# Mixer projections of two layers as three reduced-precision products each, their weights split in place, with the time step apart and some loads and softmax steps reordered

## The reference

```python
for l in range(DEPTH):                       # DEPTH = 2
    x = x + 0.5 * swiglu_ffn(rms_norm(x, ffn1_norm[l]), ffn1_w_in[l], ffn1_w_out[l])
    h = rms_norm(x, mix_norm[l])             # [256, 1024]
    uv, c_q, c_kv, k_rope, z, xbc, dt_raw, gates = jnp.split(h @ w_in[l], IN_OFFSETS, axis=-1)
    y_a = gmlp_mixer(uv, ...)                # u, v: 512 columns each
    y_b = mla_mixer(c_q, c_kv, k_rope, ...)  # 384, 256, 32 columns; 8 heads, causal softmax
    y_c = ssd_mixer(z, xbc, dt_raw, ...)     # 512, 1024, 8 columns
    g = jax.nn.sigmoid(gates).reshape(bsz, s, 3, 1024)
    merged = g[:, :, 0] * (y_a @ w_branch[l, 0]) + g[:, :, 1] * (y_b @ w_branch[l, 1]) + g[:, :, 2] * (y_c @ w_branch[l, 2])
    x = x + merged @ w_out[l]
    x = x + 0.5 * swiglu_ffn(rms_norm(x, ffn2_norm[l]), ffn2_w_in[l], ffn2_w_out[l])
```

## Time and profile before

| | us |
|---|---|
| median of 3 runs (1914.6 to 1919.06) | 1916.91 |
| the profiled execution | 1915.92 |
| its span | 1914.2 |
| mixers of layer 0, u done to the last plain gate (224 to 404) | 180 |
| the same in layer 1 (893 to 1074) | 181 |

### The profile page before, as it was taken

The page is one execution under the profiler, slowest core; times in us unless marked ns, Lnnn a source line. Parts: engine busy times, 40 slices in busy tenths (PEclk is TensorE's granted clock), DMA queues, the critical chain, the costliest instruction groups (busy, mean ns, idle before and its releaser), DMA issues.

```text
span 1914.2 us, 25859 instructions
## 1 busy us (share of the span) xinstructions
PE 1863.4 (97%) x10920; PEld 1537.3 (80%) x10920; DVE 932.7 (49%) x1168; ACT 708.7 (37%) x815; POOL 78.0 (4%) x145
## 2 busy tenths in 40 slices
PE   8999999998999999999999988999999999999998
PEld 8998585567999899985855677998887975759996
DVE  4545124468555445451344683546677531235553
ACT  5544113153554345441131533555123121215542
POOL 0000000000000000000000002000371100000000
PEclk9999999999999999999999999999998999999999
DMA  7547244333655645562444338646344223326471
GB/s 242 176 170 245 64 144 157 129 126 119 220 176 186 222 142 176 184 232 64 142 156 132 127 116 155 234 144 246 109 141 93 66 69 130 133 88 220 131 260 59
DMA packets 192248, 293.07 MB, mean 153 GB/s; under 512 B 7219, under 2 KB 126805, under 8 KB 192165
## 3 DMA queue, kind: packets, MB, share of 16 engines
q1 hardware_dynamic: 189908, 287.72, 44.5%
q0 software_dynamic: 1936, 4.14, 2.1%
q10 hardware_dynamic: 320, 0.01, 0.0%
HBM read 289.49 MB, written 2.36 MB: 152 GB/s over the span
## 4 chain that ended last, share of the span: by engine, by line
PE 91%; DVE 4%; ACT 2%; issue 2%; DMA 1%; SPq 0%; ACTq 0%; DVEq 0%
PE acc L224 17%; PE acc L225 17%; PE acc L226 17%; PE acc L193 15%; PE acc L270 7%; PE acc L205 3%; PE acc L2460 1%; PE acc L2768 1%; PE acc L456 1%; PE acc L252 1%; PE acc L1206 1%; ACT big L1323 1%; DMA ring<-in_ffn_w_out 1%; PE acc L2163 1%; ACT part_hi L215 1%
## 5 line engine op out<-in xcount | busy, mean ns | idle before, releaser
L224 PE MATMUL acc<-xT_hi,w_hi 128*128 128x256 f32 x1680 | 476.8, 284 | 8.9 <-issue 8.5
L225 PE MATMUL acc<-xT_lo,w_hi 128*128 128x256 f32 x1680 | 476.0, 283 | 0.0
L226 PE MATMUL acc<-xT_hi,w_lo 128*128 128x256 f32 x1680 | 476.0, 283 | 0.0
L424 DVE TENSOR_TENSOR w_lo<-ring,w_hi 128x2048 fp32r<-128x2048 f32 x160 | 361.8, 2290 | 222.7 <-ACT w_hi L420 222.7
L420 ACT ACTIVATE w_hi<-ring 128x2048 fp32r<-128x2048 f32 x160 | 301.2, 1912 | 160.6 <-PE acc L226 98.1
L224 PEld LDWEIGHTS acc<-xT_hi,w_hi 128*128 128x128 f32 x1680 | 323.2, 192 | 9.7 <-issue 8.7
L225 PEld LDWEIGHTS acc<-xT_lo,w_hi 128*128 128x128 f32 x1680 | 323.2, 192 | 0.0
L226 PEld LDWEIGHTS acc<-xT_hi,w_lo 128*128 128x128 f32 x1680 | 323.1, 192 | 0.0
L193 PE MATMUL acc<-ring,xT 128*128 128x512 f32 (+2 forms) x672 | 274.6, 567 | 0.8 <-DVE xT L2748 0.8
L193 PEld LDWEIGHTS acc<-ring,xT 128*128 128x128 f32 x672 | 127.3, 191 | 138.0 <-issue 125.5
L224 PE MATMUL acc<-w_hi,hT_hi 128*128 128x512 f32 x440 | 172.4, 392 | 0.1
(11 more groups left out here) (507 smaller groups left out, 2121.6 us busy)
## 6 DMA issues: line engine op xcount, KB each, us to landing
ring<-in_ffn_w_in SPq DMA_DIRECT2D x88, 1024.0 KB, 5.7
ring<-in_w_in SPq DMA_DIRECT2D x48, 1024.0 KB, 5.1
ring<-in_ffn_w_out SPq DMA_DIRECT2D x44, 1024.0 KB, 6.4
ring<-in_w_branch SPq DMA_DIRECT2D x12, 1024.0 KB, 4.9
ring<-in_w_out SPq DMA_DIRECT2D x12, 1024.0 KB, 5.0
ring<-in_w_gate SPq DMA_DIRECT2D x11, 1024.0 KB, 5.3
ring<-in_w_up SPq DMA_DIRECT2D x11, 1024.0 KB, 6.5
ring<-in_w_down SPq DMA_DIRECT2D x11, 1024.0 KB, 6.1
```

Source lines behind the costliest of these rows:

```text
L224: pe.matmul(o, a_hi, wh, start=start, stop=False)
L225: pe.matmul(o, a_hi, wl, start=False, stop=False)
L226: return pe.matmul(o, a_lo, wh, start=False, stop=stop)
L424: vec.tensor_tensor(w_part(w_lo, r), raw_part(c0, r), w_part(w_hi, r).bitcast(F32), ALU.subtract).then_inc(f.lo, 1)
```

## The change

In both layers v, c_q, c_kv, xbc, z and gates 0 to 4 are no longer plain products but `three`. For this

- ACT copies the high part of each of 20 chunks (`early_act`) into one of four slots of `early_hi`, from gate 0 on into one of three of `gate_hi`; DVE writes the rest over the raw weights (`early_vec`). Gate 4 goes the way that gate 5 went (`gate_pe`, `part_hi`), so that two more chunks do.
- The high part of the input (`normed_hi`) is made at the start of the mixers instead of before the last gate, in the memory of `xn`; its rest is written over `xT` after u and the time step are done, so both of these stay plain. For v the products with the high part of the input stand ahead of those with its rest (`early_first_pe`).
- The 8 columns of the time step come by a load of their own (`dt_in`, a sixteenth in `params_sync`), and `dt_pe` stands right behind u.
- ACT and DVE steps are cut up and put in another order round the splits; the squares of the attention's norm go from DVE to ACT (`qs_squares_act`); `qs_vec5(1)` stands right behind `qs_vec5(0)`, ahead of two splits and a gate product.
- POOL's loads wait for the 8th high part of FFN2, and the four large ones for the 11th, 14th, 17th and 20th.

The diff, cut:

```diff
-        part_hi = over_big("part_hi", 21056, RING, 4, 512)
-        normed_hi = over_big("normed_hi", 19008, KD, TOK)
+        part_hi = over_big("part_hi", 21504, RING, 4, 512)
+        normed_hi = nc.alloc_sbuf_tensor_at("normed_hi", [P, KD, TOK], F32R, offset=xn_at)
+        early_hi = over_big("early_hi", 14912, RING, 2048)
+        gate_hi = [over_big(f"gate_hi{i}", off, 2048) for i, off in enumerate((14912, 16960, 6144))]
+        dt_in = sb("dt_in", [P, KD, 8])
...
-            C_SPLIT = C_GATE + 10
+            C_SPLIT = C_GATE + 8
...
+                sync.dma_start(dt_in[:, :, :], lay("w_in", l)[:, :, COLS["dt"]:COLS["dt"] + 8]
+                               .rearrange("o (k p) n -> p (o k) n", p=P)).then_inc(par_in, 16)
...
+            early = Counters(hi=sem(f"early_hi_ready{l}"), lo=sem(f"early_lo_ready{l}"))
+            EARLY = [(c + i, n) for c, n in ((C_V, 512), (C_CQ, QR), (C_KV, KVR + ROPE), (C_XBC0, 512), (C_XBC1, 512), (C_Z, 512),
+                                             *((C_GATE + 2 * g, 512) for g in range(4))) for i in range(2)]
+            N_PROJ = 12
...
+            def early_part(e):
+                hi = early_hi[:, e % RING] if e < N_PROJ else gate_hi[(e - N_PROJ) % 3]
+                n = EARLY[e][1]
+                return hi[:, 0:4 * n].rearrange("p (k n) -> p k n", k=4)
+            def early_act(act, *es):
+                for e in es:
+                    c, n = EARLY[e]
+                    wait_chunk(act, c)
+                    if e == 1:
+                        wait_products(act, C_MIX - 1)
+                    if e == N_PROJ + 2:
+                        act.wait_ge(gm.pe, 4)
+                    if e >= N_PROJ:
+                        wait_products(act, c - 3 if e >= N_PROJ + 3 else C_XBC1 + 1)
+                    act.activation(early_part(e), slot(c, 4, n), ACT.Copy).then_inc(early.hi, 1)
+            def early_vec(vec, *es):
+                for e in es:
+                    c, n = EARLY[e]
+                    vec.wait_ge(early.hi, e + 1)
+                    vec.tensor_tensor(slot_lo(c, 4, n), slot(c, 4, n), early_part(e).bitcast(F32), ALU.subtract).then_inc(early.lo, 1)
+            def early_chunk_pe(pe, G, m, e, i, products=None):
+                c, n = EARLY[e]
+                pe.wait_ge(early.lo, e + 1)
+                if i == 0 and products != 1:
+                    wait_acc_free(pe, G, m)
+                o, ms = acc[bank(G, m)][:, 0:n], slice(m * P, (m + 1) * P)
+                for k in range(4):
+                    xh, xl = normed_hi[:, 4 * i + k, ms], xT_rest[:, 4 * i + k, ms]
+                    wh, wl = early_part(e)[:, k, :], slot_lo(c, 4, n)[:, k, :]
+                    if products == 0:
+                        pe.matmul(o, xh, wh, start=(i == 0 and k == 0), stop=False)
+                        pe.matmul(o, xh, wl, start=False, stop=False)
+                    elif products == 1:
+                        ins = pe.matmul(o, xl, wh, start=False, stop=(i == 1 and k == 3))
+                    else:
+                        ins = three(pe, o, xh, xl, wh, wl, i == 0 and k == 0, i == 1 and k == 3)
+                if m == MT - 1 and products != 0:
+                    ins.then_inc(products_done, 1)
+            def early_group_pe(pe, G, e):
+                for i in range(2):
+                    for m in range(MT):
+                        early_chunk_pe(pe, G, m, e + i, i)
+            def early_first_pe(pe, G, e):
+                pe.wait_ge(tail.act, 1)
+                for i in range(2):
+                    for m in range(MT):
+                        early_chunk_pe(pe, G, m, e + i, i, 0)
+                pe.wait_ge(tail.vec, 1)
+                for i in range(2):
+                    for m in range(MT):
+                        early_chunk_pe(pe, G, m, e + i, i, 1)
+            def early_turned_pe(pe, G, e):
+                for i in range(2):
+                    c, n = EARLY[e + i]
+                    pe.wait_ge(early.lo, e + i + 1)
+                    for f in range(4):
+                        fs, o = slice(f * P, (f + 1) * P), acc[bank(G, f // 2)][:, (f % 2) * TOK:(f % 2 + 1) * TOK]
+                        if i == 0 and f % 2 == 0:
+                            wait_acc_free(pe, G, f // 2)
+                        for k in range(4):
+                            ins = three(pe, o, early_part(e + i)[:, k, fs], slot_lo(c, 4, n)[:, k, fs], normed_hi[:, 4 * i + k, :],
+                                        xT_rest[:, 4 * i + k, :], i == 0 and f % 2 == 0 and k == 0, i == 1 and f % 2 == 1 and k == 3)
+                    ins.then_inc(products_done, 1)
...
-                w_in(C_XBC1, "xbc1", 520)
+                w_in(C_XBC1, "xbc1", 512)
...
+                pe.wait_ge(dts.vec, 2)
...
-            def dt_pe(pe, m):
-
-                pe.wait_ge(cq.vec, 6)
-                for k in range(KD):
-                    ins = pe.matmul(turn[m][:, 0:8], xT[:, k, m * P:(m + 1) * P],
-                                    slot(C_XBC1 + k // 4, 4, 520)[:, k % 4, 512:520], start=(k == 0), stop=(k == KD - 1))
-                ins.then_inc(dts.pe, 1)
-
-            def dt_vec(vec):
+            def dt_pe(pe):
+
+                for m in range(MT):
+                    for k in range(KD):
+                        ins = pe.matmul(turn[2 + m][:, 0:8], xT[:, k, m * P:(m + 1) * P], dt_in[:, k, :], start=(k == 0), stop=(k == KD - 1))
+                    ins.then_inc(dts.pe, 1)
...
             def normed_act(act):
-                act.wait_ge(sd.pe, 11)
+                act.wait_ge(mix_norm.vec, mix_norm.turned(3))
                 act.activation(normed_hi[:, :, :], xT[:, :, :], ACT.Copy).then_inc(tail.act, 1)
-                act.wait_ge(qs.vec, 23)
-                act.wait_ge(sd.vec, 24)
-                act.wait_ge(sd.pe, 13)
             def normed_vec(vec):
                 vec.wait_ge(tail.act, 1)
-                wait_products(vec, C_SPLIT - 1)
+                wait_products(vec, C_U + 1)
+                vec.wait_ge(dts.pe, 2)
                 vec.tensor_tensor(xT_rest[:, :, :], xT[:, :, :], normed_hi[:, :, :].bitcast(F32), ALU.subtract).then_inc(tail.vec, 1)
+            def tail_slots_act(act, n):
+                if n == 0:
+                    act.wait_ge(qs.vec, 23)
+                    act.wait_ge(sd.vec, 20)
+                    act.wait_ge(sd.pe, 13)
+                else:
+                    act.wait_ge(sd.vec, 26)
...
-                group_pe(pe, G_V, C_V, xT, (4, 4), 512)
-                group_pe(pe, G_CQ, C_CQ, xT, (4, 4), QR)
+                dt_pe(pe)
+                early_first_pe(pe, G_V, 0)
+                early_group_pe(pe, G_CQ, 2)
                 gm_mix_pe(pe)
-                group_pe(pe, G_KV, C_KV, xT, (4, 4), KVR + ROPE)
-                turned_group_pe(pe, G_XBC0, C_XBC0, xT, 4, 512)
+                early_group_pe(pe, G_KV, 4)
+                early_turned_pe(pe, G_XBC0, 6)
                 cq_pe(pe)
-                turned_group_pe(pe, G_XBC1, C_XBC1, xT, 4, 520, between=dt_pe)
+                early_turned_pe(pe, G_XBC1, 8)
                 gm_turn_pe(pe)
-                group_pe(pe, G_Z, C_Z, xT, (4, 4), 512)
+                early_group_pe(pe, G_Z, 10)
                 sd_cs_pe(pe)
                 qs_groups_pe(pe)
                 sd_rows_pe(pe)
-                gate_pe(pe, 0)
+                early_group_pe(pe, G_GATE, 12)
                 sd_turn_pe(pe)
-                gate_pe(pe, 1)
+                early_group_pe(pe, G_GATE + 1, 14)
                 sd_y_pe(pe)
-                gate_pe(pe, 2)
+                early_group_pe(pe, G_GATE + 2, 16)
                 sd_off_pe(pe)
-                gate_pe(pe, 3)
+                early_group_pe(pe, G_GATE + 3, 18)
                 sd_out_pe(pe)
                 qs_turn_pe(pe)
                 gate_pe(pe, 4)
                 qs_scores_pe(pe)
-                pe.wait_ge(tail.vec, 1)
-                for i in range(2):
-                    for m in range(MT):
-                        ins = split_chunk_pe(pe, tail, G_GATE + 5, m, C_SPLIT + i, i, normed_hi[:, 4 * i:4 * i + 4],
-                                             xT_rest[:, 4 * i:4 * i + 4], part_hi, i == 0, i == 1)
-                    ins.then_inc(products_done, 1)
+                gate_pe(pe, 5)
...
-                gm_act(act)
-                cq_act(act)
+                early_act(act, 0)
+                normed_act(act)
+                early_act(act, 1)
+                gm_act(act, G_U, C_U, u_s)
+                early_act(act, 2, 3)
+                gm_act(act, G_V, C_V, v_s)
+                gm_norm_act(act)
+                early_act(act, 4, 5)
+                cq_act(act, 0)
+                early_act(act, 6, 7)
+                cq_act(act, 1)
+                early_act(act, 8, 9)
                 xbc_act1(act, 0)
+                early_act(act, 10)
                 softplus_act(act, dts, dtw, 16, 2)
+                early_act(act, 11)
                 xbc_act1(act, 1)
                 xbc_act2(act)
```

(58 more changed lines are left out.)

104 lines of the change are left out of this document (60 added, 44 removed).

## The result

| | us | ratio to before, 95% interval |
|---|---|---|
| before, median of 4 runs | 1917.17 | |
| changed kernel, median of 4 runs (1848.75 to 1850.56) | 1849.32 | 0.9648, 0.9631 to 0.9664 |
| its profiled execution (its span) | 1848.8 (1847.1) | |

All executions counted here are in the fast state; one of `e8_two_products` (2480.15 us at a clock of 0.65) was in the slow state and is left out.

The account below looks back on a forecast made before the run. PE's products were taken to bound the layers' mixers (PE busy 97% of the span). 53.2 - 4.4 + 2.0 + 5.8 + 10.0 - 4.5 = 62.1 us off 1915.9 gave 1853.8 us, own range 1846 to 1862, 8 in 10 within 1844 to 1871.

Parts of the forecast that it names:

- The products: Mixers, v to gate 4: three products each instead of plain ones save 26.6 us a layer, 53.2 for both.
- Whether the splits keep up: Mixers: ACT's and DVE's splits fit beside their other work, but late places lose 2.2 us a layer, -4.4.
- The thin places: Mixers: first chunk of xbc, second chunks of gates 3 and 4, early by only 0.8, 1.3 and 1.8 us.
- The rival that DVE is late all along: Mixers: every second of 20 chunks finds its split 1 us late, a layer loses 10 us: 1874 us; chance 0.13.
- The rival of the slots that turn too slowly: Mixers: four slots without a second buffer hold PE up, slower than before, past 1925 us; chance 0.03.
- The input's rest: End of mixers: made long before, so PE's wait of 1.0 us a layer goes, +2.0 for both layers.
- The softmax: Softmax transposes: 2.4 of 4.4 us of waiting stay; 2.0 + 0.9 a layer gained, +5.8 (0 to 12.4).
- I take half: Behind the softmax: whether the clock still falls is open; half of its 1.8 us counted, 0.9 a layer.
- POOL's loads: Layer 1's FFN2: PE's 8.54 us idle and 1.5 of slow clock go, +10.0, lower bound 0.
- The load of the time step: FFN1's first output chunks: 1024 pieces of 32 bytes delay them 3.0 us; 3.5 and 1.0 lost, -4.5 (0 to -8).
- The rival with 8 us for each FFN1: The time step's load is as bad as POOL's burst, each FFN1 stands about 8 us: 1866 us; chance 0.08.
- `dt_pe` keeps its products and only moves: Time step's products, placed behind u: unchanged, so no gain or loss counted for them.

Follow-up runs that it names:

- e8_two_products: Changed kernel without the product of the input's rest with the weights' high part from c_q to gate 3: 1840.76 us, one profiled execution.
- e7: Changed kernel with an extra same-size DVE pass ahead of each of the 20 early splits: 1898.40 us, 0.9905.
- e2: Changed kernel with the softmax's second multiplication back behind a split and a gate product: 1855.80 us, 0.9677.
- e4: Changed kernel with the copies of the turned softmax ahead of the tail's last split and the second gate product on DVE: 1843.64 us, 0.9614.
- e6: Kernel before with only POOL's loads spread as in the changed kernel: 1908.57 us, 0.9948.
- e1: Changed kernel with POOL's waits as before the change: 1860.04 us, 0.9703.
- e10: Changed kernel with softmax copies first, half the time step's products between u's tiles, and POOL's loads spread more: 1839.65 us, 0.9582.
- e3: Changed kernel with the time step's load made four times, three into spare buffers: 1851.81 us, 0.9652.
- e11: Changed kernel with the time step's 16 products made twice, into the same accumulators: 1867.78 us, 0.9733.
- e12: Changed kernel measured once more, unedited: 1851.93 us, 0.9654.

## Why the prediction was right, and where it was off

The sum was 62.1 off, the profiled executions differ by 67.1, the medians of the runs by 67.9. By its own terms:

- **The products**, 26.6 a layer: right. Groups of 48 take 11.10 us (forecast 11.05), and the stretch from u to the scores is 26.4 us shorter in layer 0; in layer 1 it is 24.9, with a slow clock of 1.7 in it. The row of 0.230 us decided rightly against the Trainium skill's figure (TensorE: Matmul & The Clock Gate, "Wait — 56ns, not 53.3ns?"), by which a group would take 10.4 (an estimate by that section's formula): in the changed kernel too the trace has 0.231 to 0.233 a product.
- **Whether the splits keep up**, 2.2 lost a layer: 2.0 too much. The thin places held: gate 3's second split ended at 355.11, and PE, which began that gate at 350.82, came to the chunk half a group later, at 356.4: 1.3 us early, just as the walk had it. PE was busy for 154.00 of 154.00 us. Only `sd_out_pe` shows a trace of lateness, its 8 transposes took 1.26 us instead of 1.04. The rival that DVE is late all along didn't come true, but its mechanism is what comes next: doubled passes (e7) bring exactly those waits, and with two products (e8) they take back most of the gain. The rival of the slots that turn too slowly fell: PE waits for no chunk.
- **The input's rest**, 1.0 a layer: from the scores to the transposes 28.66 us have become 27.44 in layer 0, 1.2, and 28.68 have become 27.42 in layer 1.
- **The softmax**, 2.9 a layer: from the first transpose to the branch behind them 8.11 us have become 5.30 in layer 0, 2.8, and 7.85 have become 4.99 in layer 1, 2.9; there the slow clock behind them is gone as well. The wait went from 4.4 to 2.1 and stands where the prediction put it, at the copies; e2 and e4 show that the order of DVE alone makes it. "I take half" of the slow clock was a little low: it falls in 11 of 16 layers behind this wait.
- **POOL's loads**, 10.0: measured 8.8 in the trace, 9.2 alone (e6), 10.7 where it is undone (e1). Eleven of the 13 small loads take 14 to 23 us to land, and one slot's load beside them takes 27.2; behind it PE still waits 1.3 us, and with the small loads spread too (e10) no longer.
- **The load of the time step**, 4.5 lost: this step failed. Nothing was lost in layer 1, and the 0.3 us by which u of layer 0 starts later are within what executions differ by (206.74 to 208.12 in the traces of both kernels and the experiments). The forecast wait of some 3 us at the start of the output half isn't there. The changed kernel's transfers and splits, to be read against the earlier trace rows:

```profile
DMA packets 2006, 0.95 MB, mean 159 GB/s; under 512 B 1776, under 2 KB 1776, under 8 KB 2006
```

```profile
140.12 1.92 ACT L421 ACTIVATE w_hi<-ring 128x2048 fp32r<-128x2048 f32 x1 [2.50 <-DMA ring<-in_ffn_w_out]
143.18 1.92 ACT L421 ACTIVATE w_hi<-ring 128x2048 fp32r<-128x2048 f32 x1 [1.14 <-DMA ring<-in_ffn_w_out]
146.71 0.60 ACT L515 ACTIVATE big<-acc 128x512 f32<-128x512 f32 x1 [1.61 <-PE acc L227]
```

1776 - 725 = 1051 more packets under 512 bytes than before pass in 132:138, so each piece of 32 bytes is a packet of its own, and the chunks behind them land no later (ACT splits them at 140.12 and 143.18, before at 140.64 and 144.64). The 666 packets in 2.7 us of the earlier trace rows were no limit of the queues: 774 pass in 133:134 alone. So the step took for a rate what was only asked for; by 774 a microsecond the load is 1.3 us long, an estimate. The rival with 8 us for each FFN1 fell further: e3 has 4096 pieces and costs 2.5 us, if anything. The Trainium skill asks for 512 bytes or more a transfer for the full rate (DMA: Bandwidth & Descriptors, "Specifications"). The runs don't speak against that, but at this place 1024 pieces below it cost nothing that can be told.
- **"`dt_pe` keeps its products and only moves"**: this was wrong, and the profiled execution hid most of it. Behind u, 16 products of 8 columns bring a slow clock of 1.7 us in 12 of 18 layers, some 2.3 us an execution; in the trace it is the window 868:872 above. The prediction had put this at nothing; e11 and the table show that the products bring it on. That the profiled execution had it in one layer alone is chance; e12 has it in layer 0.

Piece by piece, both layers together, against the table of starts (a plus is better than forecast):

| piece | forecast | measured | difference |
|---|---|---|---|
| u to the scores: products and splits | 48.8 | 51.2, with 1.7 of slow clock in layer 1 | +2.4 |
| scores to transposes: the input's rest | 2.0 | 2.5 | +0.5 |
| transposes to FFN2: the softmax | 5.8 | 6.7 | +0.9 |
| FFN2 of layer 1 to the second block: POOL | 10.0 | 8.8 | -1.2 |
| the time step's load | -4.5 | -0.3 | +4.2 |
| second block to the end | 0 | -1.9 | -1.9 |

Together this is 4.9 of the 5.0 us by which the profiled execution is better than the sum. So the total came out close partly by luck: 4.1 us for the splits and 4.2 for the load that weren't lost stand against 1.7 of slow clock, 1.2 at POOL and 1.9 in the second block. Of these last 1.9 us some 1.7 are the slow clock at 1330:1335, which five of 14 traces have.

## What to carry to other kernels

Sum the busy time of the engines that feed PE, but read how close the kernel is to its next bound from their longest serial stretches: here DVE had 28% of its time free, and of 31 us less work a layer PE could use only 5, with waits and the slow clock behind them taking 14 us each. A wait of PE of 2.1 us cost its length and, in 11 cases of 16 here, some 1.7 us of slow clock more, so such a wait is worth moving one step in another engine's order. Before pricing a transfer by a rate, check in the trace that the queues were asked for more than they moved.

## What the runs showed of the hardware

- The clock falls without a wait just ahead: 16 products of 8 columns are followed by it in 12 of 18 layers, and 32 run into it, at 0.50 with PE busy without a break.
- The same program has the slow clock at a place in one execution and not in the next, at 1.7 us each: behind a wait of 2.1 us in 11 of 16 cases, behind one of 2.4 us at another place in 5 of 14.
- 1024 pieces of 32 bytes delayed nothing that can be told, and 3072 more delayed the first 1 MB load behind them by about 1 us. Eleven of POOL's 13 small loads, of 0.5 to 24 KB, took 14 to 23 us to land, and a 1 MB load issued beside them took 27.
